# Value products of the attentions with the values as the stationary operand, shares turned and spread, and a weight ring of seven split in place

## The reference

```
p = softmax(s)            # over the keys
o = einsum('bhqk,bkhd->bqhd', p, v)
```

## Time and profile before

| | us |
|---|---|
| median of 3 runs | 1712.12 (1709.77 to 1712.38) |
| the profiled execution's own time | 1713.44 |
| its span, first to last instruction | 1712.2 |
| PE busy | 1344.3 (79%) |
| DVE busy | 616.9 (36%) |
| ACT busy | 418.6 (24%) |
| mean granted clock of TensorE | 0.895 of full speed |

### The profile page before, as it was taken

How to read it: one execution, slowest core, us unless ns; L and a number is a source line. 1 busy time by engine, 2 the same in 40 slices (tenths; PEclk the granted TensorE clock), 3 DMA queues, 4 the chain that set the end, 5 groups by cost and what they waited for, 6 DMA issues and landing times.

```text
span 1712.2 us, 20375 instructions
## 1 busy us (share of the span) xinstructions
PE 1344.3 (79%) x8952; PEld 917.7 (54%) x8952; DVE 616.9 (36%) x821; ACT 418.6 (24%) x569; POOL 9.8 (1%) x64
## 2 busy tenths in 40 slices
PE   8999877676555756565665556689999999999998
PEld 8999724142212212221221222159888889998886
DVE  5667401001100101010010101047866676776665
ACT  5754400000000000000000000045534435444441
POOL 2000000000000000000000000000000000000000
PEclk9999889888877888887787878789999999999999
DMA  9545899999999999999999999994656655355560
GB/s 302 176 155 209 323 411 428 428 428 427 428 428 427 428 428 427 428 427 428 428 427 428 428 427 427 421 307 164 200 175 197 206 188 172 103 168 175 194 214 32
DMA packets 132233, 540.07 MB, mean 315 GB/s; under 512 B 8528, under 2 KB 90800, under 8 KB 108080
## 3 DMA queue, kind: packets, MB, share of 16 engines
q1 hardware_dynamic: 132128, 538.76, 79.6%
q10 hardware_dynamic: 16, 0.00, 0.0%
HBM read 537.69 MB, written 1.05 MB: 315 GB/s over the span
## 4 chain that ended last, share of the span: by engine, by line
PE 51%; DMA 36%; DVE 5%; ACT 4%; SPq 3%; issue 2%; DVEq 0%; ACTq 0%
DMA big<-in_w_dram 36%; PE bank L1779 9%; PE bank L2112 8%; PE bank L104 7%; PE bank L106 7%; PE bank L105 7%; PE bank L1808 4%; PE bank L2113 4%; SPq L95 3%; ACT hi_b L321 1%; DVE lo_b L335 1%; PE bank L1124 1%; PE bank L592 1%; PE bank L555 1%; PE bank L1741 1%
## 5 line engine op out<-in xcount | busy, mean ns | idle before, releaser
L1779 PE MATMUL bank<-big,xe 128*32 128x512 f32 x1984 | 281.1, 730 | 259.1 <-DMA big<-in_w_dram 259.1
L1779 PEld LDWEIGHTS bank<-big,xe 128*32 128x32 f32 x1984 | 77.1, 131 | 461.1 <-issue 461.1
L335 DVE TENSOR_TENSOR lo_b<-raw_b,hi_b 128x2048 fp32r<-128x2048 f32 x90 | 205.6, 2291 | 105.9 <-ACT hi_b L321 105.9
L1871 DVE TENSOR_TENSOR x<-bank,x 128x512 f32<-128x512 f32 x60 | 41.5, 691 | 524.4 <-PE bank L1723 524.4
L2112 PE MATMUL bank<-xT,hi_b 128*128 128x512 f32 x576 | 204.3, 398 | 0.0
L321 ACT CAST hi_b<-raw_b 128x2048 fp32r<-128x2048 f32 x91 | 172.8, 1904 | 20.4 <-PE bank L106 20.4
L1808 PE MATMUL bank<-big,gT 128*32 128x512 f32 x936 | 130.1, 706 | 51.9 <-DMA big<-in_w_dram 51.9
L2113 PE MATMUL bank<-xT,lo_b 128*128 128x256 f32 x576 | 161.7, 281 | 0.0
L2112 PEld LDWEIGHTS bank<-xT,hi_b 128*128 128x128 f32 x576 | 108.2, 188 | 26.4
L2113 PEld LDWEIGHTS bank<-xT,lo_b 128*128 128x128 f32 x576 | 108.8, 189 | 0.6
L1808 PEld LDWEIGHTS bank<-big,gT 128*32 128x32 f32 x936 | 36.1, 127 | 131.5 <-issue 131.5
(11 more groups left out here) (340 smaller groups left out, 2179.7 us busy)
## 6 DMA issues: line engine op xcount, KB each, us to landing
big<-in_w_dram SPq DMA_DIRECT2D x190, 2048.0 KB, 20.4
raw_b<-in_w_ffn_in_dram SPq DMA_DIRECT2D x44, 1024.0 KB, 5.1
raw_b<-in_w_ffn_out_dram SPq DMA_DIRECT2D x22, 1024.0 KB, 5.1
raw<-in_w_in_dram SPq DMA_DIRECT2D x15, 1024.0 KB, 9.2
raw_b<-in_b_w_in_dram SPq DMA_DIRECT2D x10, 1024.0 KB, 5.1
raw_b<-in_w_mix_out_dram SPq DMA_DIRECT2D x8, 1024.0 KB, 5.6
raw_b<-in_a_w_in_dram SPq DMA_DIRECT2D x7, 1024.0 KB, 12.3
raw<-in_w_out_dram SPq DMA_DIRECT2D x4, 1024.0 KB, 5.1
```

The costliest lines, as they stand in the source:

```text
L335: dve.tensor_tensor(self.lo[i % NRAW], self.raw[i % NRAW], self.hi[i % NH].bitcast(F32), ALU.subtract).then_inc(*self.s_lo.up(i))
L1779: last = pe.matmul(hb.t[32 * e:32 * e + 32, :], xe[:, k, 32 * e:32 * e + 32], each[e][k // 4][:, k % 4 * 512:(k % 4 + 1) * 512], start=(k ...
```

## The change

- *Value product.* The values are stationary (128 keys by 64 columns) and turned p moves (128 queries). Even heads write partitions 0 to 63 and odd heads 64 to 127 of the output bank, one after the other. The product of a pair of units is issued at once, at the first one's step + 4. The output has the head's columns on the partitions and the queries along the row, as the next product needs it, so it is not turned any more.
- *Division.* The reciprocal now has to stand along the row. DVE takes it at the last unit's step + 2; ACT spreads it over 64 columns for each head at + 3 (`spread`); PE turns that at + 3 (`share`), after its fill and ahead of the value products; ACT copies it out at + 4 (`share_out`), and DVE multiplies the output by it at + 4. ACT rounds the upper half from SBUF at + 4, DVE subtracts at + 5, in the first block not before step 11.
- *Order.* DVE's fill goes to the end of its step. The sigmoids go from step 11 to step 12. The ring of turned p grows from two to three buffers. The three attentions share one set of semaphores.
- *Ring.* Seven raw buffers in place of six; `lo` is written over raw, and the three `lo` buffers go. A load waits until PE has used the chunk seven before it. The second expert slot no longer overlaps the weights' buffers; the others wait for `used` in place of `lo`, the third is loaded after the fourth, and the memory tokens and the chunk after them wait for the lower halves of swa0 and swa1.
- *vrow* is turned after the forget sums, and DVE's copy follows the angles.

```diff
-NR = 6
+NR = 7
@@ Weights.load
         if i >= NR and i - NR >= self.split:
-            sp.wait_ge(*self.s_lo.of(i - NR))
+            sp.wait_ge(*self.s_used.of(i - NR))
@@ Weights.lower
-            dve.tensor_tensor(self.lo_[i % NB][:, 0:k], self.raw_[self.slot(i)][:, 0:k],
+            dve.tensor_tensor(self.lo_[self.slot(i)][:, 0:k], self.raw_[self.slot(i)][:, 0:k],
@@ Attention
+    def done(self, step, after, hold=0):
+
+        for u in range(len(self.units)):
+            if self.last(u) and max(u + after, hold) == step:
+                job = self.units[u][0]
+                yield u, job, self.out_at[job.name]
@@ pe_attend
         for go in fill.get(step, ()):
             go()
...
+        for u, job, n in a.done(step, 3):
+            b = ps.take(("share", n), a.s_share_out, n)
             pe.wait_ge(*b.was)
+            pe.wait_ge(*a.s_spread.of(n))
+            for c in range(0, job.heads * 64, P):
+                last = pe.transpose(b.t[:, c:c + P], a.scaled(n)[:, c:c + P], ident[:, :])
+            last.then_inc(*a.s_share_turned.up(n))
+        if a.pair_at(step - 4):
...
+            each = [(h, a.turned(u), i * job.width) for u in two for i, h in enumerate(a.units[u][1])]
+            for side in zip(*([x for x in each if x[0] % 2 == odd] for odd in range(2))):
+                for kt in range(job.nkt):
+                    for h, pt, at in side:
+                        last = pe.matmul(o[rows64(h % 2), h // 2 * P:(h // 2 + 1) * P], job.value(h, kt),
+                                         pt[:, at + kt * P:at + (kt + 1) * P], start=(kt == 0), stop=(kt == job.nkt - 1))
@@ act_attend, after the exponentials of the step's pair
+        for u, job, n in a.done(step, 3):
+            act.wait_ge(*a.s_share.of(n))
...
+            act.copy(a.scaled(n)[:, 0:job.heads * 64].rearrange("p (h d) -> p h d", d=64),
+                     job.rc.unsqueeze(2).broadcast_to([P, job.heads, 64])).then_inc(*a.s_spread.up(n))
+        for u, job, n in a.done(step, 4):
+            act.wait_ge(*a.s_share_turned.of(n))
+            act.copy(a.scaled(n)[:, 0:job.heads * 64], ps.of(("share", n))[:, 0:job.heads * 64]).then_inc(
+                *a.s_share_out.up(n))
         for go in fill.get(step, ()):
             go()
@@ dve_attend
+        for u, job, n in a.done(step, 2):
...
+            dve.reciprocal(job.rc, job.sm).then_inc(*a.s_share.up(n))
+        for u, job, n in a.done(step, 4):
+            dve.wait_ge(*a.s_value.of(a.base + u))
+            dve.wait_ge(*a.s_share_out.of(n))
+            z = a.scaled(n)[:, 0:job.heads * 64]
+            dve.tensor_tensor(z, ps.of(("o", n))[:, 0:job.heads * 64], z, ALU.mult).then_inc(*a.s_o_out.up(n))
@@ sp_first
-        for i in range(2, NS):
+        for i in (3, 2, *range(4, NS)):
             free(i)
             self.load_m(sp, i)
@@ act_first
-        fill.update({5: [rotated], 11: [sigmoids], 13: [split], 15: [split]})
+        fill.update({5: [rotated], 12: [sigmoids], 13: [split], 15: [split]})
```

More of the change, by code:

```diff
@@ L505, with __init__ @@
 class Attention:
-    def __init__(self, s, tag, buf, jobs, base, n_out, hold=0, late=0):
-        self.jobs, self.base, self.hold, self.late = jobs, base, hold, late
+    def __init__(self, s, buf, jobs, base, n_out, hold=0):
+        self.jobs, self.base, self.hold = jobs, base, hold
         self.p, self.pt, self.o = buf
         self.units = [(job, hs) for job in jobs for hs in job.units]
[L513 to L520, removed]
+        self.out_at = {job.name: n_out + i for i, job in enumerate(jobs)}
+        self.end, self.n_out = base + len(self.units), n_out + len(jobs)
+        (self.s_score, self.s_masked, self.s_peak, self.s_exps, self.s_share, self.s_spread, self.s_share_turned, self.s_share_out, self.s_p_turned,
+         self.s_p_out, self.s_value, self.s_o_out, self.s_o_hi, self.s_o_lo) = (s[n] for n in (
+             "score", "masked", "peak", "exps", "share", "spread", "share_turned", "share_out", "p_turned", "p_out", "value", "o_out", "o_hi", "o_lo"))
     def steps(self):
-        return range(len(self.units) + 4)
+        return range(len(self.units) + 5)
     def last(self, u):
@@ L527, in last, with pair_at, turned, scaled @@
         return hs is job.units[-1]
[L529 to L536, removed]
+    def pair_at(self, step):
+        two = range(step, min(step + 2, len(self.units)))
+        return two if step % 2 == 0 and step >= 0 else ()
+    def done(self, step, after, hold=0):
[3 more added lines that the diff above has]
+                yield u, job, self.out_at[job.name]
+    def turned(self, u):
+        return self.pt[(self.base + u) % 3]
+    def scaled(self, n):
+        return self.o[n % len(self.o)]
 def pe_attend(pe, ps, a, ident, fill):
-    for step in [*a.steps(), len(a.units) + 4]:
+    for step in a.steps():
         if step % 2 == 0 and step < len(a.units):
@@ L579, in pe_attend @@
-        if 0 <= step - 3 < len(a.units):
-            u = step - 3
-            job, hs = a.units[u]
-            pe.wait_ge(*a.s_p_out.of(a.base + u))
-            for i, h in enumerate(hs):
[L584 to L597, removed]
@@ new lines, in pe_attend @@
+            for c in range(0, job.heads * 64, P):
+                last = pe.transpose(b.t[:, c:c + P], a.scaled(n)[:, c:c + P], ident[:, :])
+            last.then_inc(*a.s_share_turned.up(n))
+        if a.pair_at(step - 4):
+            two = a.pair_at(step - 4)
+            job = a.units[two[0]][0]
+            n = a.out_at[job.name]
+            if n not in job.opened:
+                job.opened[n] = ps.take(("o", n), a.s_o_out, n, hold=True)
+                pe.wait_ge(*job.opened[n].was)
+            o = job.opened[n].t
+            pe.wait_ge(*a.s_p_out.of(a.base + two[-1]))
+            each = [(h, a.turned(u), i * job.width) for u in two for i, h in enumerate(a.units[u][1])]
[4 more added lines that the diff above has]
+                                         pt[:, at + kt * P:at + (kt + 1) * P], start=(kt == 0), stop=(kt == job.nkt - 1))
+            last.then_inc(*a.s_value.up(*(a.base + u for u in two)))
+            if a.last(two[-1]):
+                ps.let(("o", n))
@@ L620, in act_attend @@
         for go in fill.get(step, ()):
             go()
-        for job, k in a.ripe(step):
-            h0, nh = job.groups[k]
-            n = a.out_at[job.name, k]
+        for u, job, n in a.done(step, 4, a.hold):
             h3, _ = pair(job.put.dst)
-            act.wait_ge(*a.s_o_turned.of(n))
-            act.copy(h3[job.put.at(h0, nh, job.qt)], ps.of(("o turned", n))[:, 0:nh * 64].rearrange(
+            act.wait_ge(*a.s_o_out.of(n))
+            act.copy(h3[job.put.at(0, job.heads, job.qt)], a.scaled(n)[:, 0:job.heads * 64].rearrange(
@@ L628, in act_attend @@
                 "p (c s) -> p c s", s=P)).then_inc(*a.s_o_hi.up(n))
 def dve_attend(dve, ps, a, fill):
[L632 to L643, removed]
-                    dve.wait_ge(*a.s_masked.now())
[L645 to L658, removed]
-                        if a.last(u):
-                            dve.wait_ge(*a.s_peak.now())
-                            dve.tensor_tensor(job.rc, job.sinks[:, 0:job.heads], job.nm, ALU.add).then_inc(
-                                *a.s_sink.up(a.base + u))
@@ L990, in pe_first @@
             *s["forget_sum"].up("all"))
+        b = ps.take("vec", s["vec"], "all")
+        pe.wait_ge(*b.was)
+        pe.wait_ge(*s["vrow"].of("all"))
+        pe.transpose(b.t[:, 0:88], m.vrow[0:88, :], m.ident[0:88, 0:88]).then_inc(*s["vec_turned"].up("all"))
         self.down(w, m.hT, "v1", s["evicted"], hT)
@@ L1307, in split @@
             at[0] += 1
[L1309 to L1313 removed]
+        for i in range(5):
             split()
```

157 lines of the change are left out of this document (85 added, 72 removed).

## The result

The changed kernel takes 1725.58 us in the median of 4 runs (1721.89 to 1727.52), the kernel before 1711.76 beside it: ratio 1.0077, 95% interval 1.0065 to 1.0089, slower. The forecast was 1717, and 1725.6 lies 0.4 us inside the upper end of its range, outside the 1713 to 1721 that its own mechanism was given, and where the rival "the waits drop the clock" put 1726.

A forecast was written before the change was run, and what follows sets the result against it. The prediction took PE to bound both ends and DMA of expert weights the middle. Its terms -2.2 - 1.4 + 2.9 + 5.8 = +5.1 us gave 1717.3 on the profiled span, 1717 us for the median, range 1704 to 1726.

The forecast's parts named there:

- the waits drop the clock: Rival: PE's new waits bring half clock, two of four caught costing 8 to 10 us, 1726 us; chance 0.15.
- its own mechanism: The forecast's main case: PE waits for the shares outweigh the gains, 1713 to 1721 us; chance 0.48.
- Who waits: PE waits for ACT's spread: 5.2 us in the first memory attention; 3.6, 4.0, 3.4 at long-attention steps 12, 14, 18.
- What such a wait costs: Second block: each PE wait for the shares counted at its own length, with no clock loss in the sum.
- a granted clock that falls in the second block: One of the signs the prediction named for being wrong.
- Value products: All attentions: 232 products save 49 ns each, 11.4 us at most, less 0.2 us for each of 16 groups, 3.2 us.
- First block, -3.6 to the first expert matmul: Up to the first expert matmul: -2.2 us from moving vrow and -1.4 us from the first block's attention.
- The vrow term: First block: PE's 2.25 us wait for vrow before k0 goes, -2.2 us, bounds 0 and -2.3.
- The middle part hands an earlier start on in full: DMA-bound expert part: starting PE's expert work earlier gains as much as it starts earlier.
- Second block, +8.7: Second block's attentions: +2.9 us in the first memory attention and +5.8 us in the long one.
- Edits at nothing: Ring of seven, expert load order and ACT's 28 extra copies, about 12 us: no effect on time beyond ACT's order.

The follow-up runs named there:

- e_first: Changed kernel with ACT's spread of the reciprocals ahead of the step's exponentials in all three attentions; 1714.11 us, 1.0013 to the kernel before.
- e_all: Changed kernel, spread ahead of exponentials, memory attention's ACT split and GELUs behind it, long attention's step-17 split at 18, table load at the end; 1709.04 us.
- e_dummy: Changed kernel with 34, 21, 29 and 24 useless identity transpositions on PE ahead of its four long waits for the spread shares; 1716.36 us.
- e_apart: e_best with each head's value products together instead of even and odd heads in turn; 1710.56 us, 0.9994 to the kernel before.
- e_vrow: Kernel before with only vrow's transposition moved behind the forget sums and DVE's copy behind the angles; 1710.94 us, 0.9992.
- e_fill: e_final with 16 matmuls of ones on PE in its wait for DVE's routing sums ahead of the first expert; 1700.20 us, 0.9931.
- e_six: Changed kernel with a ring of six weight buffers instead of seven, still split in place; 1724.07 us, 1.0075 to the kernel before.
- e_final: e_best with the early spread in the second block only and DVE's step-13 split in the long attention at step 15; 1700.03 us, 0.9935.
- e_best: e_all with DVE's reciprocal ahead of its copy of turned scores, spread one step earlier, DVE's second memory-attention split at step 6; 1707.28 us, 0.9982.

## Why the prediction came out as it did

- *Who waits.* Right in place and size: forecast 5.2, 3.6, 4.0 and 3.4 us, measured 4.7, 3.0, 4.0 and 3.3. e_first and e_all moved only what stood in front of the spread, and the waits in the second block shrank from 15.0 to 8.7 and 5.9 us.
- *What such a wait costs.* **This is the step that failed.** I priced each wait at its own length and gave the clock 0.15, with the argument that none of the waits of 1 us in the second block moved it. Those were no measure for waits of 3 to 5 us; the row that was, with its 2.4 us wait, showed the fall, and I used it only for the rival. The trace of the kernel before had another, at the start of the second block, which I overlooked:

```profile
1136.20 1.49 PE L2034 MATMUL bank<-ident,x 128*128 128x128 f32 x8 [1.98 <-DVE x L2542]
```

```profile
1137.20:1144.00 6.80, 5.74 (x27) 5.37 (x26) 6.76 (x9) 4.57 (x5) 0.00 (x0) 0.50 1.09 351
```

All four new waits were followed by half clock, 10.1 us by the windows; e_dummy took back 9.2 with the shares as late as before. The prediction had named a granted clock that falls in the second block as a sign of being wrong, and it fell.
- *That the time lies in the range is luck in part.* The range reached to 1726 for the clock rival's sake. The rival's own number was reached by other terms: it counted two of the four waits caught, each with ten us at half clock, 4 to 5 us lost; all four were caught, with 3.4 to 7 us of half clock each, 1.7 to 3.2 us lost.
- *Value products.* Mechanism right (e_apart), size too large. A group of 16 took 1.77 us before (two of 0.84 to 0.93); now 1.02, plus 0.10 at the two transpositions in front (0.31 from their start to the group's against 0.21) and 0.15 at the four behind (0.59 against 0.44): 0.50 saved, where 16 x 49 ns less 0.2 gave 0.58. A group of 8 takes 0.59 + 0.25 against 0.88 and saves next to nothing. With 13 groups of 16 and 3 of 8 that is 6.5 us instead of 8.2. Going in and out of the form costs 0.4 us a group, not the 0.2 that I read from one side of L2226.
- *First block, -3.6 to the first expert matmul.* Measured -3.3. The first transposition of x came 1.1 us later (8.43 against 7.31), because the 26 opening matmuls on ones, the same in both, took 5.67 instead of 4.54 us in that execution; without this it is -4.4. Of these 2.1 are vrow's by e_vrow, so the attention gave some 2.3 instead of 1.4, by one execution of each kernel. No wait over 1 us arose at the shares there, as forecast. The vrow term holds as a mechanism; its worth in the new kernel is larger, since the old place with the new ring would cost 8.4 us.
- *The middle part hands an earlier start on in full.* In the changed kernel it gave 2.3 us more. From the first expert matmul to the combination the thirteen profiled executions took 917.6 to 922.3 us, so one execution can't tell 2 us here; the 1.0 us of e_fill was not to be seen in the medians.
- *Second block, +8.7.* Measured +18.6: 15.0 of waits and 10.1 of clock, less 6.5 for the products and old small waits (forecast 7.9); this last term is what is left over and was not measured by itself. With the clock's 10 us added to the forecast 1717 the sum would have been 1727.
- *Edits at nothing.* e_six bears out the ring; ACT's extra copies cost only by their order: e_final has all of them, and its second block waits 0.5 us for the shares.

## What to carry to other kernels

A wait put on the bounding engine is priced twice: its length, and what the engine does at half clock behind it. Here waits of 2.4 us and more in the two attentions and before the routing sums were followed by it, and at times shorter ones, so a trace of the kernel before is worth searching for every wait with a lower clock behind it. Before adding a small operation to a chain (here a 0.35 us spread), list for every queue that it passes what is issued ahead of it; clearing one queue shows the next, and an operation moved forward delays what now stands behind it. Issue the small operation in the first step in which its input is ready, unless something that ends last stands behind it, as the rotated keys did in e_best.

## What was not expected of the hardware

The length of a wait alone doesn't tell whether the clock falls. PE's waits of 2.4 us before the routing sums, of 2.5 us in e_all and of 2.0 us in the kernel before (at 1136.2) were followed by half clock, and so were the 1.2 and 0.4 us of e_best, one shortly after the other. The wait of 2.0 us at the end of e_all's long attention and that of 2.25 us for vrow in the kernel before were not, while one of 2.2 us for the rotated keys in e_apart was. In e_fill, with PE kept busy before the routing sums, the clock stayed up there. The stretch of half clock was 3.4 to 10.2 us long, and in equal code it differed: step 18's wait of 3.3 us had 6.8 us behind it in the changed kernel and 3.4 in e_first. Transpositions alone, 34 in a row over 3.9 us with 1.0 us of waiting behind them, kept the clock at 1.00 in e_dummy.
